# Weight sums of a seven-product block multiplication made by accumulating transfers, and the seventh product's weights split ahead of the sixth's

## The reference, cut to what matters

```
h = rmsnorm(x) * (1 + scale) + shift
proj = h @ w_in                       # 1024 x 1024 times 1024 x 10240, float32
glu_a, glu_b, z_conv, q, k, v, z_att, g_conv, g_att = split(proj)
u = causal_conv31(glu_a * sigmoid(glu_b)); ...
att = three groups of dilated window attention over q, k, v
```

## Time and profile before

| | us |
|---|---|
| median of 3 runs | 2522.97 (2519.49 to 2524.65) |
| the profiled execution, its own time | 2521.86 |
| its span, first to last instruction | 2520.1 |
| PE busy | 2446.9 |
| DVE busy | 1574.7 |
| ACT busy | 887.5 |
| POOL busy | 828.6 |

### The profile page before, as it was taken

One profiled execution on the slowest core, in us unless ns is written; L12 is line 12 of the kernel. 1 busy time (PEld: TensorE's weight loads), 2 busy tenths in 40 slices (PEclk: granted clock), 3 DMA queues, 4 the chain that ended last, 5 costly groups with the idle time before them and its releaser, 6 DMA issues.

```text
span 2520.1 us, 31982 instructions
## 1 busy us (share of the span) xinstructions
PE 2446.9 (97%) x11800; PEld 2013.6 (80%) x11800; DVE 1574.7 (62%) x3034; ACT 887.5 (35%) x1722; POOL 828.6 (33%) x797
## 2 busy tenths in 40 slices
PE   7999999999999999989999999999999999999997
PEld 4787788987889887878888878878887787887875
DVE  8714678777787785573674611124477857768788
ACT  5214331133311333550132133321165455355453
POOL 3435554336643475243244222224210000000000
PEclk9999999999999999999999999999999999999998
DMA  7527442154611758442342032225368675766854
GB/s 260 172 71 292 142 170 76 51 218 165 214 56 56 252 177 280 144 158 85 127 145 87 25 109 68 72 98 169 104 193 242 162 190 122 194 170 164 216 117 102
DMA packets 188623, 372.68 MB, mean 148 GB/s; under 512 B 22195, under 2 KB 61363, under 8 KB 178869
## 3 DMA queue, kind: packets, MB, share of 16 engines
q1 hardware_dynamic: 168548, 321.88, 37.6%
q0 software_dynamic: 18768, 44.57, 9.8%
q10 hardware_dynamic: 1152, 4.19, 0.4%
HBM read 289.65 MB, written 72.55 MB: 144 GB/s over the span
## 4 chain that ended last, share of the span: by engine, by line
PE 83%; DVE 9%; DMA 2%; ACT 2%; issue 2%; POOL 1%; SPq 0%; DVEq 0%; ACTq 0%; POOLq 0%
PE ps L2811 41%; PE ps L3068 19%; PE ps L2958 13%; PE ps L2935 3%; PE ps L2911 2%; PE ps L2921 2%; PE ps L2840 2%; DVE w_lo L2547 1%; DVE w_lo L2556 1%; POOL w_lo L1382 1%; DMA h2c_d<-late_hi 1%; DVE big L2605 1%; DVE ps L2102 0%; DVE big L2403 0%; DMA raw<-in_w_in 0%
## 5 line engine op out<-in xcount | busy, mean ns | idle before, releaser
L1380 POOL CAST w_hi<-raw 128x512 fp32r<-128x512 f32 x216 | 149.6, 693 | 714.5 <-DMA raw<-in_w_in 309.6
L2811 PE MATMUL ps<-w_hi,act_hi 128*128 128x512 f32 (+1 forms) x960 | 376.2, 392 | 1.1 <-DVE act_lo L1961 1.1
L2102 DVE SCALAR_TENSOR_TENSOR ps<-scr,small,ps 128x256 f32<-128x256 f32 x928 | 374.1, 485 | 1.0
L2811 PE MATMUL ps<-w_hi,act_lo 128*128 128x512 f32 (+1 forms) x960 | 369.5, 385 | 0.0
L2811 PE MATMUL ps<-w_lo,act_hi 128*128 128x512 f32 (+1 forms) x960 | 368.8, 384 | 0.0
L3068 PE MATMUL ps<-w_hi 128*128 128x512 f32 x896 | 350.6, 391 | 11.0 <-issue 7.5
L3068 PE MATMUL ps<-w_lo,w_hi 128*128 128x512 f32 x896 | 349.4, 390 | 0.0
L3068 PE MATMUL ps<-w_hi,w_lo 128*128 128x512 f32 x896 | 349.3, 390 | 0.0
L2811 PE MATMUL ps<-act_hi,w_hi 128*128 128x512 f32 x768 | 305.3, 398 | 12.3 <-DVE act_lo L1961 4.1
L2811 PE MATMUL ps<-act_lo,w_hi 128*128 128x512 f32 x768 | 304.4, 396 | 0.0
L2811 PE MATMUL ps<-act_hi,w_lo 128*128 128x512 f32 x768 | 301.3, 392 | 0.0
(11 more groups left out here) (279 smaller groups left out, 4039.5 us busy)
## 6 DMA issues: line engine op xcount, KB each, us to landing
raw<-in_w_in SPq DMA_DIRECT2D x136, 256.0 KB, 3.6
late_hi<-h2c_d SPq DMA_DIRECT2D x21, 1024.0 KB, 7.6
w_hi<-parts_d SPq DMA_DIRECT2D x18, 1024.0 KB, 4.9
w_lo<-parts_d SPq DMA_DIRECT2D x18, 1024.0 KB, 7.8
raw_c<-in_w_in SPq DMA_DIRECT2D x27, 512.0 KB, 4.9
vreg<-in_w_ada SPq DMA_DIRECT2D x36, 256.0 KB, 5.6
raw<-in_w_in SPq DMA_DIRECT2D x18, 512.0 KB, 5.2
raw<-in_w_up POOLq DMA_DIRECT2D x8, 1024.0 KB, 11.8
```

The source lines that it names most:

```text
L1380: pool.tensor_copy(dhi, src).then_inc(w_hi_done, 1)
L2102: nc.vector.scalar_tensor_tensor(dst[:, here], u_in[:, there], w[:, j:j + 1], ps_c[:, here], ALU.mult, ALU.add).then_inc(tap, 1)
L2811: ins = nc.tensor.matmul(out_, lhs, rhs, start=(m == 0), stop=(m == 3 * nk - 1))
```

## The change

- POOL no longer adds. Four times a block it issues a transfer that adds a weight quarter from DRAM to a raw buffer (`block_add`): a += W01, b += W11, a += W11, a += W10. Two semaphores count them, `sum_a` (the former `t_sum`) and `sum_b` (`t4_part`, whose later counts are shifted by `T4_PART0`).
- c is loaded twice a block (W10, W11), and the load at j = 4 goes. Its first load waits for the former block's split of product 3.
- `T_ORDER` becomes 1, 2, 5, 7, 6, 3, 4: the split of product 7 goes ahead of those of 6 and 3. PE's own order is the same. By the ring, the split of 6 now waits for product 1 of the same block, that of 3 for product 2; in the earlier order the splits of 6, 3 and 7 waited for the former block's product 4 and for products 1 and 2.

```diff
-T_ORDER = (1, 2, 5, 6, 3, 7, 4)
+T_ORDER = (1, 2, 5, 7, 6, 3, 4)
...
                 elif j:
                     sp.wait_ge(t_split, split_count(n, 2))
-                elif t_loads[2] % 3 == 0:
-                    if n:
-                        sp.wait_ge(t_sum, 4 * n)
-                else:
-                    sp.wait_ge(t_split, split_count(n, 3))
-                    sp.wait_ge(t_sum, 4 * n + 3)
+                elif n:
+                    sp.wait_ge(t_split, split_count(n - 1, 3))
...
-                if j == 4:
-                    block_load(n, 2, 1, 0)
...
-            def block_sum(n, i, dst, other):
-
-                pool.wait_ge(t_split, 14 * n + (4, 6, 8, 12)[i])
-                if i >= 1:
-                    pool.wait_ge(t_sum, 4 * n + i)
-                pool.tensor_tensor(dst, dst, other, ALU.add).then_inc(t_sum, 1)
+            def block_add(dst, src, signal):
+                pool.dma_start(dst, src, accum_op=ALU.add).then_inc(signal, 16)
 
             def block_weights(n):
 
                 a, b, c = t_raw
+                sum_a, sum_b = t_sum, t4_part
                 pool.wait_ge(t_ld[0], T_LD0[0] + 16 * (n + 1))
                 block_split(n, 1, a)
-                pool.wait_ge(t_ld[2], T_LD0[2] + 16 * (3 * n + 1))
+                pool.wait_ge(t_split, split_count(n, 1))
+                block_add(a, block_weight(n, 0, 1), sum_a)
+                pool.wait_ge(t_ld[2], T_LD0[2] + 16 * (2 * n + 1))
                 block_split(n, 2, c)
                 pool.wait_ge(t_ld[1], T_LD0[1] + 16 * (n + 1))
-                block_sum(n, 0, a, b)
-                pool.wait_ge(t_sum, 4 * n + 1)
+                block_add(b, block_weight(n, 1, 1), sum_b)
+                pool.wait_ge(sum_a, 16 * (3 * n + 1))
                 block_split(n, 5, a)
-                pool.wait_ge(t_ld[2], T_LD0[2] + 16 * (3 * n + 2))
-                block_sum(n, 1, a, c)
-                pool.wait_ge(t_sum, 4 * n + 2)
+                pool.wait_ge(t_split, split_count(n, 5))
+                block_add(a, block_weight(n, 1, 1), sum_a)
+                pool.wait_ge(sum_b, 16 * (n + 1))
+                block_split(n, 7, b)
+                pool.wait_ge(sum_a, 16 * (3 * n + 2))
                 block_split(n, 6, a)
-                block_sum(n, 2, b, c)
+                pool.wait_ge(t_split, split_count(n, 6))
+                block_add(a, block_weight(n, 1, 0), sum_a)
+                pool.wait_ge(t_ld[2], T_LD0[2] + 16 * (2 * n + 2))
                 block_split(n, 3, c)
-                pool.wait_ge(t_sum, 4 * n + 3)
-                block_split(n, 7, b)
-                pool.wait_ge(t_ld[2], T_LD0[2] + 16 * (3 * n + 3))
-                block_sum(n, 3, a, c)
-                pool.wait_ge(t_sum, 4 * n + 4)
+                pool.wait_ge(sum_a, 16 * (3 * n + 3))
                 block_split(n, 4, a)
```

More of the change, by code:

```diff
@@ L185 @@
 FORMS = 9
+FRESH = 4
 def block_unit(g, i):
@@ L425, in build @@
         form_ld, FORM_LD0 = ada_ld[3:6], [16 * ADA_SLOT.count(i) for i in range(3, 6)]
-        pfree = on_a + on_c + [t_hi, t_split, t_sum, block_done]
-        PFREE0 = [4 * 3 * NG] * 2 + [3 * 3 * NG] * 2 + [14 * 3 * NG] * 2 + [4 * 3 * NG, 14 * 3 * NG]
+        pfree = on_a + on_c + [t_hi, t_split, form_lo, block_done]
+        PFREE0 = [4 * 3 * NG] * 2 + [3 * 3 * NG] * 2 + [14 * 3 * NG] * 2 + [FRESH, 14 * 3 * NG]
+        T4_PART0 = 16 * 3 * NG
         form_st, FORM_ST0 = {"s1": const_ld, "s2": pos_ld, "s3": row_out, "s4": ada_mm}, {
@@ L599, in build @@
         FORM_DRAM = {"s1": 0, "s2": 1, "s3": 2, "s4": 3, "a21": 4}
-        FRESH = 4
         def form_part(place, part):
@@ L1328, in _ @@
                     sp.wait_ge(wc_lo, 2 * at_product(blk, 7) + 2)
-                    sp.wait_ge(t4_part, 16 * (blk + 1))
+                    sp.wait_ge(t4_part, T4_PART0 + 16 * (blk + 1))
                     weight_load(blk + 1, 1)
@@ L1468, in _ @@
                 weight_add(0, weight_quarter(blk, 1, 1), t2_sum)
-                pool.wait_ge(t4_part, 16 * (blk + 1))
+                pool.wait_ge(t4_part, T4_PART0 + 16 * (blk + 1))
                 weight_add(2, weight_quarter(blk, 0, 0), t4_sum)
```

## The result

The changed kernel takes 2530.31 us in the median (2527.79 to 2533.59, 4 runs), the kernel before 2521.8 us in the runs taken beside it (2519.49 to 2524.65, 4 runs). The ratio is 1.0034, with a 95% interval of 1.0021 to 1.0047: slower, by more than a measurement of this kernel leaves open. The time lies in the range, 2517 to 2534, but it is rival B's, not that of the forecast of no change. The profiled execution of the changed kernel is the fastest of its four, 2527.79 us with a span of 2526.0: 5.9 us longer than before. The medians lie 8.5 us apart; the traces can show 5.9 us of that and no more.

The account below looks back on a forecast made before the run. PE was taken to bound the kernel, busy 2446.9 of 2520.1 us; every term summed to 0 on its path, so the profiled execution stays at 2521.9 and the median, 1.1 above, is 2523.0 us; range 2517 to 2534.

Parts of the forecast that it names:

- rival B: Buffer a's sums land late, so PE waits at product 6, blocks 7, 8, 5: 2526.5 to 2535.9 us; chance 0.20 from L 10.2.
- the forecast of no change: Whole kernel: POOL's work hidden before and after, 2523.0 us; 0.67 within 0.2%, B's small form included.
- D: DVE, freed of POOL's sums, is on time at block starts: all 8.2 us back, 2514.8; chance 0.08.
- C: Form loads late behind adding transfers: 0.7 us a block from two in front, 6 us in nine blocks, 2529; chance 0.05.
- one landing crowded and one quiet: Buffer a's two sums: first lands in 9.8 us beside the form load, second in 5.4 after it.
- the chain through buffer a: Splits and sums before product 6: block 7's half split done at 889.5, wanted at 891.51, 2.0 us to spare.
- the 17.2 that I had allowed: Block 7: most that the landings of a's two sums may total, in us, within the 27.0 allowed.
- that one is issued after the split of product 2, about 874, and has 8 us: Block 7: the transfer into b leaves about 874 and has 8 us to land before product 7's split.
- if the transfer into b has landed: Condition for product 7's split to lie inside a's second transfer's flight (882.1 to 886); order change put at 0.
- 4L - 35.7 us: B's cost in blocks 7 and 8 together, for a mean landing L of a's sums.
- threshold of 10.2 us: Mean landing from which B decides; there it costs 5 us in blocks 7 and 8.
- the chances, 0.67 against 0.20: 0.67: time within 0.2%, B's small form included; 0.20: slower by B, landings from 10.2 us on.

Follow-up runs that it names:

- second experiment: Changed kernel with the old order of splits (1, 2, 5, 6, 3, 7, 4), all sums still by transfers; 1.0042, 2532.94 us.
- The repeated run: The changed kernel itself, unaltered, timed again beside the other runs; 1.0039, 2532.25 us over 5 runs.
- first experiment: Kernel before with only the order of splits changed to 1, 2, 5, 7, 6, 3, 4, sums still on POOL; 1.0038, 2531.3 us.
- third's: Changed kernel with 6144 bytes in place of 4096 for the memory describing POOL's transfers; 1.0017, 2525.71 us over 11 runs.

## Why the prediction was wrong, and where it was right

**Right.** Nothing is gained by relieving POOL, and the 8.2 us that PE waits for DVE stay (7.7): D did not happen. No product waited for a form (C), though the second half of a form load took 11.1 us in block 7 and 11.2 in block 8, where 8.0 was read. Quiet sums land in 5.7 to 6.1 us, the forecast was 5.4; the median of the 36 is 6.7, inside the 5.4 to 9.8 named. The page's row for POOL's transfers in the stages (KB each, median us to landing):

```profile
raw<-in_w_in POOLq DMA_DIRECT2D x36, 512.0 KB, 6.7
```

The DMA shares of the stages rose by 14, 14 and 13 points where 18 were forecast, and POOL's busy time fell by 42.6 us where "about 30" was, mostly since an issue took 1310 ns, less than both nearest groups; 36 of them are 47.1 us. The order of tightness (block 7, 8, 5) was read from the right rows, though block 8 came out worst.

**The step that failed** is "one landing crowded and one quiet" in the chain through buffer a. The numbers of it, block 7 and block 8 of the profiled execution:

| step | forecast | block 7 | block 8 |
|---|---|---|---|
| split 1 and gap to the issue | 3.9 | 4.3 | 4.3 |
| first sum | 9.8 | 5.7 | 9.2 |
| b's issue ahead of split 5 | 0 | 1.1 | 1.2 |
| split 5 and gap | 3.9 | 4.7 | 4.7 |
| second sum | 5.4 | 11.0 | 10.1 |
| half of split 6 | 1.95 | 1.95 | 1.95 |
| total, with gaps of 0.25 | 25.0 | 29.0 | 31.6 |
| room, by rows of before | 27.0 | 27.0 | 28.3 |

Two things are wrong with it. First, the second sum was priced quiet, because the form load would have landed by then. In block 7 the two landings sum to 16.7 us, more than the 15.2 forecast, yet within the 17.2 that I had allowed; in block 8 they are 19.3 against 18.5. The crowd had only moved. In block 7 the second half of the form load landed at 882.4, 1.9 us after a's second sum had left; in block 8 it landed at 934.2, 2.1 us before that sum left, and the sum still took 10.1 us. Behind the form load SP issues result stores and the reload of c (872.46 to 874.99), and b's sum, which I took for a bystander with 8 us of flight, itself takes 11.8 us and stands in the same queue ahead of a's second. What each of these adds was not separated. With b's sum a block early a's second still took 10.2 and 9.1 us, with smaller form loads 8.9 and 7.1, so b's place in the queue looks like the smaller part. In every kernel with full form loads the second sum of these blocks took 9.0 to 11.8 us. The quiet price was right for a quiet landing, and in these two blocks the second landing was not one.

Second, some 2.6 us of POOL's own were left out of the chain: 0.3 to 0.4 us between a split and an issue, b's issue of 0.8 us between a's landing and the split that waits for it, and 0.5 us by which the cast behind each issue is slower. The issues were in the sum as busy time, worth nothing there, and not in the chain, where they count in full. By landings alone block 7 would have been in time (16.7 in 17.2). With 2.6 us on top it is 2.0 us over its room. PE was itself 0.65 us later than before when the stage began, so 1.4 us remain, the wait of 1.39 that PE shows. With the forecast's own landings, 15.2 us, it would have been 0.6 over.

The step "that one is issued after the split of product 2, about 874, and has 8 us" failed too: 875.00 in block 7, but in block 8 4.4 us after that split, and in block 5 7.2 us. In block 5 it decides. a's second sum had landed by 643.3, but the split of product 7 waits for b's landing, and the split of product 6 comes behind it (POOL in time):

```profile
640.58 0.61 POOL L1387 CAST w_hi<-raw 128x512 fp32r<-128x512 f32 x1 [2.44 <-DMA raw<-in_w_in]
...
644.41 0.61 POOL L1387 CAST w_hi<-raw 128x512 fp32r<-128x512 f32 x1
```

So the 1.0 us of block 5 are not the chain through a, as B had it, but b's landing in front of product 7's split in the new order, which the forecast had put at 0 "if the transfer into b has landed". The second experiment's kernel, with the old order, loses nothing in block 5.

**What the range owes to B.** B was priced at 4L - 35.7 us for blocks 7 and 8. The mean landing of the four is 9.0 us, by which B would cost 0.3. It cost 5.0 and, with the clock below, 6.7. So B's mechanism and kind of price were right in these two blocks, and its threshold of 10.2 us was 1.3 us too high, a quarter of the 5.2 us that were missing in two blocks. With them, both landings at 9.8 would have cost 3.5 + 5.2 = 8.7 us, which no longer counts as no change: the chances, 0.67 against 0.20, came in good part from that omission. That the time lies in the range is no merit of the forecast: the range had been stretched up to 2534 for B. Its lower end was given as half of D, which would be 2518.9; 2517 stands for 6.0 of D's 8.2 us.

**What stays open.** The three kernels with b's sum early are still 0.07 to 0.10% above the kernel before, at the edge of what their intervals exclude; block 8 costs 1.0 to 1.4 us in their profiled executions, and the rest was not separated. No version tried is faster than the kernel before. None could be by this term: before the change no block product waited for POOL.

## What to carry to other kernels

An operation taken off a resource that does not bound the kernel can still sit on a loop, here of buffer a: load, split, sum, split, sum, split. Add up that loop's latencies for one period, with the issuing engine's own gaps and issues in it and each landing at its crowded value, those of transfers queued ahead included, and compare with the period. If such a transfer must be used, issue it as soon as its buffer is ready, and not between two that the loop needs; where it has to stand there, give the descriptor memory room for both (1.0017 here instead of 1.0034).

## What the runs showed of the hardware that was not expected

**Small packets beside large ones.** The adding transfers travel in packets of 1 KB, the form loads in packets of 8 KB. The queues of the changed kernel in two windows of 1 us, 924 to 925 and 927 to 928 (packets, MB, share of the 16 engines):

```profile
q0 software_dynamic: 156, 0.16, 103.9%
...
q1 hardware_dynamic: 49, 0.40, 96.3%
q0 software_dynamic: 19, 0.02, 12.2%
```

While the other queue moves nothing the adding transfer gets 156 packets in a microsecond, and beside the form load 19, against 49 of the other queue. In bytes that is a twentieth. So it stands nearly still while the form load passes, which fits a landing time that depends so much on when it starts. In the 4 us behind b's issue in block 7, 876 to 880, its queue moves no packet at all and the other 150. That the engines take turns by packets and not by bytes is my reading of these counts, not shown.

**Descriptor memory makes an issue wait for a landing.** With 4096 bytes the second of two adding transfers left 0.3 us after the landing of the first, in every block but the first one; with 6144 bytes it left as soon as POOL reached it, while the first was in flight.

**An idle PE comes back slower.** The further 1.65 us in product 6 of block 8 are clock. Windows of PE in the changed kernel (window, length, busy and instructions, granted clock, DMA share, GB/s):

```profile
938.00:942.00 4.00, 4.00 (x21) 1.00 1.17 259
942.00:945.00 3.00, 3.00 (x23) 1.00 0.86 142
945.00:948.00 3.00, 0.31 (x1) 1.00 0.03 4
948.00:952.00 4.00, 3.47 (x9) 0.61 0.09 31
952.00:956.00 4.00, 4.00 (x20) 0.96 0.99 163
```

PE is idle for 3.2 us after a long busy stretch, and the next 4 us are granted 0.61, a mean of the upper level and mostly the lower one, 1.2 GHz. The matmuls follow one another at 0.43 us instead of 0.235:

```profile
949.62 0.63 PE L2952 MATMUL ps<-w_hi 128*128 128x512 f32 x1
950.04 0.63 PE L2952 MATMUL ps<-w_hi,w_lo 128*128 128x512 f32 x1
```

The repeated run has it too (0.67 over 948 to 952 us, after a wait of 2.8 us). The length of the wait alone does not decide it. In the first experiment's kernel PE waited 2.45 us in block 7, in the third's 2.52 us in block 8. The first was slowed, and lost 1.6 us more inside product 6, the other was not (the same columns, the four microseconds behind each wait; first experiment, then third):

```profile
895.00:899.00 4.00, 3.92 (x15) 0.64 0.00 0
```

```profile
946.40:950.40 4.00, 3.70 (x15) 1.00 0.02 4
```

In the second experiment's kernel, after 4.2 us of waiting, the next 4 us were all at the lower level, and 2.8 us more were lost:

```profile
897.00:901.00 4.00, 3.63 (x13) 0.50 0.00 0
```

So a stall can be billed a second time, here by half to two thirds of its own length. The Trainium skill, page TensorE: Matmul & The Clock Gate, section Part 1 on the clock gate, says that the clock is set by how busy PE has been recently; the trace agrees, with 0.61 behind the idle stretch and 1.00 ahead of it. What sets the two waits of 2.5 us apart, no run here shows.
